# Second block's last norm of heads: a written-out order, four banks for gate products, a second place for the scales' rows, and the first gates fetched and opened there

## The reference

```
y_df = _differential_attention(...)
y_df = _rmsnorm(y_df, subln_df) * (1.0 - lam_init)
merged = (jax.nn.sigmoid(g_sb + b_gate[:D_MODEL]) * (y_sb.reshape(b, tp, -1) @ w_br_sb)
...
h = h + _mixer(...)          # merged @ w_out
h = h + _conv_ffn(...)
```

## Time and profile before

| | |
|---|---|
| median of three runs | 3006.99 us |
| profiled execution | 3007.5 us |
| its span, first to last instruction | 3005.7 us |
| TensorE busy | 95% |
| granted clock, mean | 0.980 |
| last norm of heads, from its first square to the merge's first product | 1595.65 to 1632.28 us |
| merge of the second block, first product to start of the last sum | 1632.28 to 1688.9 us |

### The profile page before, as it was taken

The page is one execution under the profiler, slowest core; times in us unless marked ns, Lnnn a source line. Parts: engine busy times, 40 slices in busy tenths (PEclk is TensorE's granted clock), DMA queues, the critical chain, the costliest instruction groups (busy, mean ns, idle before and its releaser), DMA issues. The chain is left out here.

```text
span 3005.7 us, 40245 instructions
## 1 busy us (share of the span) xinstructions
PE 2866.7 (95%) x16173; PEld 2338.0 (78%) x16173; DVE 1361.2 (45%) x2458; ACT 1134.1 (38%) x2059; POOL 1236.8 (41%) x593
## 2 busy tenths in 40 slices
PE   6999989999999979999998999999999999999998
PEld 4875558888988867777887989988787766888887
DVE  5436650341133233773552555532477542566620
ACT  4347762222244333443553422222343355422221
POOL 5432224554345432222222545554445423545553
PEclk9999999999999988999997999999999999999999
DMA  7410003222322211114223322223222223422222
GB/s 262 141 57 15 15 28 99 93 96 98 119 91 91 98 47 58 43 43 140 78 77 106 137 86 92 97 100 105 81 93 82 84 74 106 158 91 98 99 98 91
DMA packets 84377, 275.77 MB, mean 92 GB/s; under 512 B 9759, under 2 KB 10015, under 8 KB 84064
## 3 DMA queue, kind: packets, MB, share of 16 engines
q1 hardware_dynamic: 82856, 272.37, 27.2%
q10 hardware_dynamic: 1336, 0.83, 0.1%
HBM read 258.41 MB, written 17.90 MB: 92 GB/s over the span
## 5 line engine op out<-in xcount | busy, mean ns | idle before, releaser
L132 POOL TENSOR_TENSOR weights_lo<-weights_raw,weights_hi 128x1024 fp32r<-128x1024 f32 x415 | 1007.0, 2428 | 1344.1 <-ACT weights_hi L124 1343.8
L124 ACT ACTIVATE weights_hi<-weights_raw 128x1024 fp32r<-128x1024 f32 x415 | 437.6, 1058 | 1062.5 <-PE acc L491 551.5
L489 PE MATMUL acc<-h_hi,weights_hi 128*128 128x512 f32 (+2 forms) x1808 | 663.9, 367 | 27.3 <-ACT gate_tiles L2541 8.2
L490 PE MATMUL acc<-h_lo,weights_hi 128*128 128x512 f32 (+2 forms) x1808 | 638.6, 353 | 0.0
L491 PE MATMUL acc<-h_hi,weights_lo 128*128 128x512 f32 (+2 forms) x1808 | 638.4, 353 | 0.0
L489 PEld LDWEIGHTS acc<-h_hi,weights_hi 128*128 128x128 f32 x1808 | 344.9, 191 | 108.1 <-issue 51.7
L491 PEld LDWEIGHTS acc<-h_hi,weights_lo 128*128 128x128 f32 x1808 | 345.1, 191 | 45.6
L490 PEld LDWEIGHTS acc<-h_lo,weights_hi 128*128 128x128 f32 x1808 | 345.8, 191 | 41.0 <-issue 0.2
L489 PE MATMUL acc<-y_hi,weights_hi 128*128 128x512 f32 (+2 forms) x392 | 141.5, 361 | 13.3 <-DVE full L2731 6.9
L535 PE MATMUL acc<-weights_hi,h_hi 128*128 128x256 f32 (+1 forms) x480 | 144.8, 302 | 8.0 <-DVE h_lo L997 5.2
L825 ACT ACTIVATE probs<-probs,low 128x31 f32<-128x31 f32 (+5 forms) x276 | 138.5, 503 | 18.5 <-DVE low L792 18.0
(11 more groups left out here) (432 smaller groups left out, 5299.0 us busy)
## 6 DMA issues: line engine op xcount, KB each, us to landing
weights_raw<-in_stream SPq DMA_DIRECT2D x415, 512.0 KB, 3.3
weight_ring<-in_w_ada SPq DMA_DIRECT2D x24, 512.5 KB, 7.5
gates<-gate_tiles SPq DMA_DIRECT2D x24, 258.0 KB, 4.2
gate<-gates SPq DMA_DIRECT2D x8, 774.0 KB, 5.5
held<-gates SPq DMA_DIRECT2D x8, 768.0 KB, 6.0
gates<-gate_tiles SPq DMA_DIRECT2D x23, 256.0 KB, 4.1
bias_copies<-bias_rows SPq DMA_DIRECT2D x1, 3068.0 KB
table<-bias_copies SPq DMA_DIRECT2D x1, 2560.0 KB, 10.0
```

The source lines that it names most:

```text
L124: act.activation(self.hi[:, at % CUT, :], self.raw[:, at % RAW, :], ACT.Copy).then_inc(self.hi_done, 1)
L132: pool.tensor_tensor(self.lo[:, at % CUT, :], self.raw[:, at % RAW, :], self.hi[:, at % CUT, :].bitcast(F32), ALU.subtract).then_inc(self. ...
L489: pe.matmul(out, left[0], right[0], start=start, stop=False)
L490: pe.matmul(out, left[0], right[1], start=False, stop=False)
```

## The change

The norm's phase has its order written out, as counts of dense slots (D), norm (H), cut (C) and first gates (G), in place of the three paced lanes. Its dense lane has four banks, and the store of gate chunks three places instead of two. The spread scales go in turn to `wide` and to `sums`, and a spread waits for the scaling two before. The buffer of the gates is allocated before the phase; a new lane, `FirstGates`, fetches the merge's first three gate tiles when this phase starts and opens the first of them after the root. `Merge` uses its fetches and openings for the later tiles. In the third block `PackedMerge` gets `fetches = True` and a `yield` behind its three first fetches. Other users of `HeadNorm` keep one place.

```diff
@@ HeadNorm.__init__ @@
-        self.wide = psum("wide", [P, n, 512])
+        self.wide = [psum("wide", [P, n, 512]), self.sums][:sets]
@@ HeadNorm.pe @@
-            if i >= 1:
-                pe.wait_ge(self.done, i)
+            sets = len(self.wide)
+            if i >= sets:
+                pe.wait_ge(self.done, i - sets + 1)
...
@@ new class @@
+class FirstGates(Lane):
+    fetches = True
...
+    def fetch(self, sp, i):
+        sp.dma_start(self.gate[:, i % 3], self.gates[i]).then_inc(self.gate_in[i % 3], 16)
+    def open_gates(self, act, i):
+        act.wait_ge(self.gate_in[i % 3], 16 * (i // 3 + 1))
+        for branch in range(self.gate.shape[2]):
+            gate = self.gate[:, i % 3, branch]
+            act.activation(gate, gate, ACT.Sigmoid, bias=...).then_inc(self.opened, 1)
+    def sp(self, sp):
+        for i in range(3):
+            self.fetch(sp, i)
+        yield
+    def act(self, act):
+        self.open_gates(act, 0)
+        yield
@@ Merge @@
-        for i in range(3):
-            fetch(i)
...
-        open_gates(0)
...
@@ second_block @@
+        opened = inner.enter_context(home(nc, "gate", [P, 3, 3, N2 * W_OUT]))
...
-            store = GateStore(sem, sbuf, gates, GATES_A + GATES_B, N2, W_OUT)
+            store = GateStore(sem, sbuf, gates, GATES_A + GATES_B, N2, W_OUT, ring=GATES_C)
-            dense = Dense(sem, psum, ws, units, GATES_C)
-            scaled = HeadNorm(..., P, n, w)
+            dense = Dense(sem, psum, ws, units, GATES_C, banks=4)
+            scaled = HeadNorm(..., P, n, w, sets=2)
-            run.lanes(paced((dense.weights, 0, 1), (scaled.weights, 0, 0.8), (cut.weights, 0, 1), ([1], 1, 1)),
-                      [dense, scaled, cut, StoredGates(store)], 2 * KT)
+            begun = FirstGates(sem, k, opened, gates.rearrange("(b i) p t -> i p b t", b=3), gate)
+            led, D, H, C, G = [0] * (2 * KT), [0], [1], [2], [4]
+            sums = H + C + H + C + H + C + H
+            root = H + G + H + H + H + D * 4 + C + D * 20
+            spread = H + D * 3 + H + C + D * 3 + H + C + D * 2 + H + C + D + C + C
+            run.lanes(led + sums + root + spread + [3], [dense, scaled, cut, StoredGates(store), begun], 2 * KT)
```

More of the change, by code:

```diff
@@ L544, with __init__ @@
 class HeadNorm(Lane):
-    def __init__(self, sem, sbuf, psum, k, A, heads, dim, n, w, rows=P, gains=None):
+    def __init__(self, sem, sbuf, psum, k, A, heads, dim, n, w, rows=P, gains=None, sets=1):
         self.k, self.A, self.heads, self.dim, self.n, self.w, self.rows, self.gains = k, A, heads, dim, n, w, rows, gains
@@ L600, in pe @@
         for i in range(H):
-            if i >= 1:
-                pe.wait_ge(self.done, i)
+            sets = len(self.wide)
+            if i >= sets:
+                pe.wait_ge(self.done, i - sets + 1)
             for half in range(n):
                 for part in range(2):
-                    last = pe.matmul(self.wide[0:self.rows, half, 0:w], rows_of[:, i * P:i * P + self.rows],
+                    last = pe.matmul(self.wide[i % sets][0:self.rows, half, 0:w], rows_of[:, i * P:i * P + self.rows],
                                      self.parts[:, part, half * w:(half + 1) * w], start=part == 0, stop=part == 1)
@@ L628, in dve @@
             dve.wait_ge(self.spread, i + 1)
-            dve.scalar_tensor_tensor(self.flat(tile), self.flat(tile), gain, self.wide[0:self.rows, :, 0:self.w], ALU.mult, ALU.mult
+            dve.scalar_tensor_tensor(self.flat(tile), self.flat(tile), gain, self.wide[i % len(self.wide)][0:self.rows, :, 0:self.w], ALU.mult, ALU.mult
                                      ).then_inc(self.done, 1)
@@ L2604, in pool, with __init__ @@
             yield
+class FirstGates(Lane):
+    fetches = True
+    def __init__(self, sem, k, gate, gates, bias_at):
+        self.k, self.gate, self.gates, self.bias_at = k, gate, gates, bias_at
+        self.gate_in = [sem(f"gate_in{i}") for i in range(3)]
+        self.opened = sem("opened")
+    def fetch(self, sp, i):
[4 more added lines that the diff above has]
+            gate = self.gate[:, i % 3, branch]
+            act.activation(gate, gate, ACT.Sigmoid, bias=self.k.vec[:, self.bias_at + branch * KT + i:self.bias_at + branch * KT + i + 1]
+                           ).then_inc(self.opened, 1)
+    def sp(self, sp):
[5 more added lines that the diff above has]
+        yield
 class Merge(Lane):
-    def __init__(self, sem, sbuf, psum, k, ws, gates, bias_at, source, spans, out, n, w, late):
+    def __init__(self, sem, sbuf, psum, ws, begun, source, spans, out, n, w, late):
         self.late = late
-        self.k, self.ws, self.gates, self.bias_at, self.source, self.spans, self.out, self.n, self.w = k, ws, gates, bias_at, source, spans, out, n, w
+        self.ws, self.begun, self.gate, self.source, self.spans, self.out, self.n, self.w = ws, begun, begun.gate, source, spans, out, n, w
         self.first = ws.take(KT)
         self.B = len(spans)
-        self.gate_in = [sem(f"gate_in{i}") for i in range(3)]
-        self.opened, self.products_done, self.combined = sem("opened"), sem("products_done"), sem("combined")
+        self.products_done, self.combined = sem("products_done"), sem("combined")
         self.full_done, self.hi_done, self.lo_done = sem("full_done"), sem("hi_done"), sem("lo_done")
-        self.gate = sbuf("gate", [P, 3, self.B, n * w])
         self.full = sbuf("full", [P, 2, n * w])
@@ L2629, in fetch @@
         def fetch(i):
-            if i >= 3:
-                sp.wait_ge(self.full_done, (i - 2) * self.n)
+            sp.wait_ge(self.full_done, (i - 2) * self.n)
             if i == KT - 1:
                 self.late.wait_all(sp)
-            sp.dma_start(self.gate[:, i % 3], self.gates[i]).then_inc(self.gate_in[i % 3], 16)
-        for i in range(3):
-            fetch(i)
+            self.begun.fetch(sp, i)
         for i, piece, m in self.pieces():
@@ L2686, in act @@
     def act(self, act):
[L2687 to L2692, removed]
         def cut(i):
@@ L2858, in second_block @@
             first = Dense(sem, psum, ws, store.units(ws, 0, h_out), 1, acc=lead)
-            merged = Merge(sem, sbuf, psum, k, ws, gates.rearrange("(b i) p t -> i p b t", b=3), gate, lambda t: cuts.tile(t, T_OUT),
+            merged = Merge(sem, sbuf, psum, ws, begun, lambda t: cuts.tile(t, T_OUT),
                            [(SB_Q, SP_Q), (SP_Q, DF_Q), (DF_Q, KT)], out, N2, W_OUT, store)
```

6 lines of the change are left out of this document (3 added, 3 removed).

## The result

| | before | changed |
|---|---|---|
| median of the first comparison | 3006.19 us (4 runs) | 2991.17 us (4 runs, 2987.92 to 2993.3) |
| ratio, 95% interval | | 0.9942 (0.993 to 0.9954) |
| ratio in five rounds (below) | | 0.9938 (0.9924 to 0.9951) |
| profiled execution, span | 3007.5, 3005.7 us | 2993.3, 2991.5 us |

The kernel is 15 us faster in the first comparison, where 20.2 was forecast; 2991.17 lies 4.4 us over the predicted 2986.8 and inside the range. Over the four comparisons of this document the kernel before was timed 41 times, with a median of 3008.6 us, and the changed kernel 12 times, with a median of 2991.3: 17.3 us apart. The four runs of before in the first comparison, median 3006.19, lie low among the 41, so its 15 us are rather too small.

The account below looks back on a forecast made before the run. TensorE, busy 95% of the span, was taken as the bound, with gains only where it idles or its clock is down. Terms 9.5 + 8.6 + 2.1 = 20.2 us gave 2986.8 us against the 3006.99 median; range 2982 to 2996.5.

Parts of the forecast that it names:

- First wait: Second block's last head norm: four banks and the new order remove TensorE's bank wait and slow clock, 9.5 us.
- ScalarE's cover: Second block's norm: sigmoid load and openings fit inside the reciprocal's wait; 1.9 us in hand before the first spread.
- Second place at 0: Norm's spread scales alternating between two places: worth 0 to 1 us alone, taken as 0.
- the aside: Norm's spreads: without the second place, the tighter order would stall by about one scaling a head.
- The edge: Norm to merge: last store costs 4.2 us, under the lead chunk's 5.7, cover 1.6; rival of a longer wait, chance 0.08.
- Second wait: Second block's merge: earlier gate fetches remove TensorE's 6.9 us wait for VectorE's first sum and 1.7 slow clock, 8.6 us.
- The cover of 0.6 us at the first piece: Second block's merge: VectorE releases the bank at 1627.9, TensorE wants it at 1628.5.
- Third block: Its merge: first three gate fetches leave at the edge, so TensorE's whole wait for the first sum goes, 2.1 us.
- one stage only: Rival: norm or merge alone gains because a wait re-forms, losing 8.6 to 9.5 us, about 2996; chance 0.09.
- The clock in the norm: Rival: TensorE's clock drops in the second block's norm, giving 2993 us; chance 0.11.
- the swings: Norm's gate products: cycling round banks with small idles between groups lets the clock swing; same rival as the clock drop.
- The rival with ScalarE before a transfer: Norm: opening waits for gates landing after 1606.3, each microsecond lost, clock falling 2 to 7 us; slower, chance 0.03.

Follow-up runs that it names:

- e3: Kernel before with only four banks and three store places, its order, scales and gates kept: 3006.55 us, ratio 0.9992.
- e6: Changed kernel with two banks instead of four for the gate products: 2991.49 us, ratio 0.9937.
- e5: Changed kernel with one place for the spread scales instead of two: 2991.65 us, ratio 0.9935.
- e4: Changed kernel with the first gates fetched at the merge's own edge and opened behind the lead chunk: 2988.83 us, ratio 0.9937.
- e7: Changed kernel run again, nothing altered, for a second profile: 2994.52 us, one run.
- e8: Changed kernel run a third time, nothing altered, for its profile: 2991.26 us, one run.

## Why the prediction was right, and where its size was off

- **First wait, 9.5 us: right.** 21.24 us between the two products against 21.3 built from counts; the sums are 0.3 later from the head norm's first row on, not 0.2, and that row stands 0.3 later behind the edge. Measured from the edge, the gain is 9.2 us. The 0.89 us row that the prediction took for a spread at full clock was partly at the lower one: at full clock the row is 0.75. It did no harm, since a spread with its gaps took 0.88 where 0.95 was charged, and the last evacuation 0.4 where 0.3 was. e3 and e6 show that it takes both parts: banks without the order give 2.3 us, the order without four banks is 4.9 short.
- **ScalarE's cover: right.** The openings end 0.2 us before the rounding is released. The sigmoid's table load starts 0.01 us behind the root's end (1603.83), and the first opening 0.01 us behind the load. The rows decide against the 1.38 us drain that the Trainium skill's page "ScalarE: Activation LUTs", section "What ACT_TABLE_LOAD costs", adds: none is seen at the sigmoid's load here, nor at the root's in the earlier trace rows. At the root's load here the root came 0.58 us behind the load's end, with a wait for VectorE, and that too is less than the drain.
- **Second place at 0: right in the sum, wrong in the aside** that a tighter order would stall without it. In the changed kernel the scaling of a head ends 0.41, 0.39 and 0.03 us before the next spread starts (first 1612.68 and 1613.09), so the last one has almost no room; e5 has no wait.
- **The edge: right.** Store issued by 1617.5, edge at 1622.26: 4.7 us in place of 4.2, still 1.2 us ahead of the lead chunk's end.
- **Second wait, 8.6 us: right**, 8.8 measured; 18.0 for the two terms together against 18.1. The cover of 0.6 us at the first piece came out at 0.56: VectorE's last row ends at 1628.77, TensorE goes on at 1629.33. The wait itself was 5.5 to 7.6 us in the five profiles of the old gates, and the second part of the stage 31.2 to 33.5, so the term is 7.9 to 10.3 us by the execution that one starts from. A fetch takes 4.1 to 4.5 us with nothing ahead of it, not the 5.0 to 7.3 of the earlier trace rows; this only added cover here, but the expectation of e4, built on 5.8, came out 3 us too high by it and by the opening's place.
- **Third block, 2.1 us: mechanism right, size at the top** of 0.7 to 2.1. One execution's wait was read as the kernel's. The fetch at the edge took 4.3 us and not the 6.3 of the sum.
- **The step from the stages to the whole run is the one that came out short.** In the first profile the terms gave 20.5 us, where 20.2 was forecast; the kernel's time fell by 15.0 (14.2 in the profiled pair), and by 17.3 between the medians of all runs. In the profiled pair the missing 6.3 us lie in unchanged code: 5.0 in one stretch of the third block where the clock fell, 0.5 ahead of the change, the rest small. That this stretch varies is shown (0.6 in e7, e8); why the profiles with the changed stage lost 3.6 us more outside of it on average than those of the old order is not. It may belong to the change, or to the fast executions that were profiled of the old one; that stays open. My range covered it, as "one stage only", for a reason that did not occur.
- The clock in the norm stayed at 1.00, so that rival did not occur. Nor did the swings that the prediction takes from the Trainium skill's page "TensorE: Matmul & The Clock Gate", section "A second HAM failure mode: psum-queue depth-cycling": TensorE went round four banks at 1.00, with 20.89 of 21.30 us busy. The rival with ScalarE before a transfer did not occur either: the first opening had its gates 8.6 us early, where the prediction's bound was 5.0.

## What to carry to other kernels

When TensorE waits for a bank, look at what stands in front of the evacuation in ScalarE's order: here a rounding that waited for a reciprocal. More banks alone moved the wait to the next consumer of that reciprocal; banks and an order that gives TensorE 72 products to do meanwhile removed it. A fetch wanted at a phase's start belongs in front of that phase's first blocking store, and its price is to be read from a fetch that had nothing queued ahead of it (4.4 us here, not 5.8).

## What the runs showed of the hardware

- How long the clock stays low behind a wait differed with the work behind it. After 3.77 us of wait, products in a row were back at 0.12 us a step after 3.2 us (granted clock 0.88 over 14.1 us, e6). After 3.34 us (before) and 2.23 us (e3), with spreads of four rows between runs of 9 or 12 products, it took some 14 and 10 us (0.52 over 14.3 us, 0.64 over 14.1). That the spreads are the reason is not shown.
- The length of the wait alone does not tell whether the clock falls. It fell behind 2.23 us in e3; behind 2.14 us in the third merge of before (1.00 from 2551.40 to 2554.00) and behind the 1.28 us in e4 it did not.
- A first fetch of 774 KB of gates landed 4.1 to 4.5 us after its issue with nothing ahead of it, and after 5.7 to 6.2 us behind a weight load and a store. The third block's, 768 KB, took 4.3 to 4.4 and 5.8 to 6.3.
- Stretches at half clock in unchanged code come and go between executions: 5.0 us in 61 in one profile, 0.6 in the next two.
